# Unused matrix products in front of 31 of TensorE's waits, in a long one-core network kernel

## The chip, the cores and the metric

The kernel runs on one core of one Trainium2 chip, in one launch. The metric is the device time of that launch in microseconds (us), the median over its runs. TensorE (PE in the rows) does the matrix products, VectorE (DVE), ScalarE (ACT) and GpSimd (POOL) the rest; each works through its own instructions in order and waits on semaphores for the others.

## The reference

One batch of 512 positions with 1024 features goes through five layers. All arithmetic is fp32.

```python
# the first block (DEPTH = 1)
h = _rms(x, norm1_w[l]) * (1 + sc1) + sh1
x = x + g1 * _hybrid_mixer(h, ...)        # state-space scan + dilated attention + pooling
h = _rms(x, norm2_w[l]) * (1 + sc2) + sh2
x = x + g2 * (jnp.square(jax.nn.relu(h @ w_ff1[l])) @ w_ff2[l])
# the second block: four layers on 512 latent and 256 context positions
#   l = 0, 3: window attention;  l = 1: attention with low-rank q and kv;  l = 2: decayed attention
#   y_l, y_c = mixer(rmsnorm(h_l) ..., rmsnorm(h_c) ...);  each then normed, gated and added to x
def rmsnorm(x, g):
    xf = x.astype(jnp.float32)
    y = xf * lax.rsqrt(jnp.mean(xf * xf, axis=-1, keepdims=True) + EPS)
    return (y * g.astype(jnp.float32)).astype(x.dtype)
```

## The kernel before, in words

Most of the work is in `dense`: a weight matrix comes in 156 slots of 128x2048, each is split into a high part (ScalarE, line 409) and a low part (GpSimd, line 401), and each product of the reference becomes three products in TensorE's fp32r form (lines 414, 415 and 416: high by high, low by high, high by low). A tile of the output accumulates over 8 chunks of 128 features in one of the 8 PSUM banks and is taken out by ScalarE or VectorE. With `lead=2` the first two tiles of a call are built together, chunk by chunk, so that TensorE can begin when the first chunk of its input (`a_hi`, `a_lo`) has been written.

Between these calls stand stages in which TensorE has little to do:

- `pre_norm` squares each chunk of x on ScalarE (line 880), sums over the features with a product by a matrix of ones (line 896), takes the root on ScalarE (`root_rows`, lines 843 and 846, each with a load of a table), and scales and splits on VectorE and ScalarE (lines 919, 932, 905). In the second block it comes at the start of every layer, for the 512 latent columns and then the 256 context columns. `rms_scale` (lines 823 and 832) is its plain form, used twice in `ssd_out`.
- `layer_out` ends a layer: a dense product, a sum of squares (line 2239), and x plus the gated, normed y on VectorE (lines 2256 and 2264), chunk by chunk, with `pre_norm` of the next layer behind it.
- `ssd_branch` has four short stages with a barrier after each (`end_stage`: every engine drains, counts up a semaphore and waits for the others): transposes of dt (line 1046), transposes of the inputs (line 1069), the states (line 1126), and the heads (lines 1218, 1232, 1235).
- `dilated_attention` norms the heads (line 1350, ones by squares), and `group_attention` (line 1398: scores), `pair_attention` (lines 1671: scores, 1681: transposes, 1692: values), the attention of layer 1 (lines 1513 to 1536) and `decayed_attention` (lines 2936 to 2954) do the attentions.

The order on every engine is written out by hand. Products on plain fp32 operands are two instructions each in the trace (a count of x16 in a row is 8 products); those of lines 414 to 416 are one each.

## Time and profile before

| | |
|---|---|
| median of 3 runs | 3102.14 us (3098.28 to 3105.61) |
| the profiled execution's own time | 3101.86 us |
| its span, first to last instruction | 3100.1 us |
| TensorE busy | 2813.1 us (91%) |
| VectorE, ScalarE, GpSimd busy | 54%, 39%, 24% |
| mean granted TensorE clock | 0.958 of full speed |

The clock that the chip grants TensorE has two levels in the records, 1.00 (2.4 GHz) and 0.50 (1.2 GHz). A busy time of TensorE holds the work done at either. An idle time is written behind a row in brackets, with what ended it.

### The profile page before, as it was taken

The numbers are of one execution on the slowest core, as the hardware profiler recorded it, in microseconds if no ns is written. First come the engines' busy times: TensorE is split into PE (matmuls) and PEld (weight loads), VectorE is DVE, ScalarE is ACT, GpSimd is POOL, SyncE is SP. The second block draws the span as 40 slices with busy tenths as digits, with TensorE's granted clock in tenths as the row PEclk, the third lists the DMA queues.
The fourth block names the chain that finished last, engine by engine and source line by source line (L and its number), as shares of the span: only waits on it lengthen the run. The fifth ranks groups of instructions, "written<-read, shape, count | busy, mean of one in ns | idle before, by whom it ended". The sixth has DMA issues, their size and how long they took to land.

```text
span 3100.1 us, 39554 instructions
## 1 busy us (share of the span) xinstructions
PE 2813.1 (91%) x16088; PEld 2295.3 (74%) x16088; DVE 1674.2 (54%) x3104; ACT 1217.1 (39%) x2104; POOL 743.5 (24%) x160
## 2 busy tenths in 40 slices
PE   3978989989899999999989989999899999889896
PEld 1855877768687787769867768777689998768685
DVE  5877295162822999970088441354490248450583
ACT  3335224553223122242268354543443336352482
POOL 1411433403343344423200112100122210113101
PEclk7989999999899999999999999999999999989998
DMA  6412463302323554521100211101121331122101
GB/s 239 183 41 102 186 235 109 109 1 82 109 95 126 186 190 178 202 109 69 56 14 2 82 68 69 41 1 43 64 84 69 137 136 42 68 82 82 41 2 68
DMA packets 49620, 294.79 MB, mean 95 GB/s; under 512 B 4448, under 2 KB 5792, under 8 KB 19616
## 3 DMA queue, kind: packets, MB, share of 16 engines
q1 hardware_dynamic: 22464, 163.59, 14.6%
q10 hardware_dynamic: 26976, 128.68, 10.9%
q8 instruction: 128, 2.10, 0.3%
q14 instruction: 52, 0.43, 0.0%
HBM read 271.25 MB, written 21.00 MB: 94 GB/s over the span
## 4 chain that ended last, share of the span: by engine, by line
PE 63%; DVE 18%; ACT 4%; issue 3%; DMA 0%; ACTq 0%; DVEq 0%
PE psum L414 16%; PE psum L415 15%; PE psum L416 15%; DVE ada_temp L748 5%; PE psum L1671 2%; PE psum L896 2%; PE psum L2954 2%; PE psum L1513 2%; PE psum L1536 2%; PE psum L1692 1%; DVE pair_row L1721 1%; PE psum L1681 1%; PE psum L1517 1%; PE psum L1525 1%; DVE pair_prob L1730 1%
## 5 line engine op out<-in xcount | busy, mean ns | idle before, releaser
L401 POOL TENSOR_TENSOR w_lo<-raw,w_hi 128x2048 fp32r<-128x2048 f32 x156 | 743.3, 4765 | 2314.3 <-ACT w_hi L409 2314.3
L414 PE MATMUL psum<-a_hi,w_hi 128*128 128x512 f32 (+3 forms) x1880 | 708.1, 377 | 78.4 <-DVE a_lo L905 54.2
L415 PE MATMUL psum<-a_lo,w_hi 128*128 128x512 f32 (+3 forms) x1880 | 698.8, 372 | 0.0
L416 PE MATMUL psum<-a_hi,w_lo 128*128 128x512 f32 (+3 forms) x1880 | 698.1, 371 | 0.0
L414 PEld LDWEIGHTS psum<-a_hi,w_hi 128*128 128x128 f32 (+1 forms) x1880 | 356.7, 190 | 156.1 <-issue 56.8
L748 DVE SCALAR_TENSOR_TENSOR ada_temp<-ada_ring,ada_rows 128x1024 f32<-128x1024 f32 x240 | 426.7, 1834 | 78.8 <-ACT ada_rows L708 46.3
L415 PEld LDWEIGHTS psum<-a_lo,w_hi 128*128 128x128 f32 (+1 forms) x1880 | 357.2, 190 | 63.3 <-issue 4.2
L416 PEld LDWEIGHTS psum<-a_hi,w_lo 128*128 128x128 f32 (+1 forms) x1880 | 356.6, 190 | 63.3 <-issue 2.2
L409 ACT ACTIVATE w_hi<-raw 128x2048 fp32r<-128x2048 f32 x156 | 298.1, 1912 | 250.5 <-DMA raw<-stream 105.6
L414 PE MATMUL psum<-w_hi,a_hi 128*128 128x256 f32 x800 | 229.6, 287 | 0.5 <-ACT c_gate_rows L2830 0.5
L416 PE MATMUL psum<-w_hi,a_lo 128*128 128x256 f32 x800 | 226.3, 283 | 0.0
L415 PE MATMUL psum<-w_lo,a_hi 128*128 128x256 f32 x800 | 226.3, 283 | 0.0
L414 PEld LDWEIGHTS psum<-w_hi,a_hi 128*128 128x128 f32 x800 | 153.4, 192 | 2.4 <-issue 1.4
L415 PEld LDWEIGHTS psum<-w_lo,a_hi 128*128 128x128 f32 x800 | 153.5, 192 | 1.5 <-issue 1.4
L416 PEld LDWEIGHTS psum<-w_hi,a_lo 128*128 128x128 f32 x800 | 153.5, 192 | 0.0
L2226 DVE TENSOR_TENSOR square<-y 128x512 f32<-128x512 f32 (+1 forms) x56 | 44.8, 800 | 179.6 <-ACT y L2232 179.6
L1721 DVE CUSTOM_DVE_ANT_0 pair_row<-psum,pair_mask,neg_sinks 128x512 f32<-128x512 f32 (+2 forms) x160 | 116.6, 747 | 38.3 <-PE psum L1671 25.3
L1749 ACT ACTIVATE pair_prob<-pair_row,pair_stat 128x513 f32<-128x513 f32 (+2 forms) x160 | 114.8, 719 | 42.3 <-DVE pair_stat L1721 21.9
L896 PE MATMUL psum<-squares,const 128*128 128x512 f32 (+1 forms) x160 | 79.7, 658 | 39.6 <-ACT squares L880 39.3
L1671 PE MATMUL psum<-gk,gq 64*128 64x128 f32 (+1 forms) x960 | 98.7, 340 | 18.2 <-DVE pair_stat L1721 14.5
L414 PE MATMUL psum<-hid_hi,w_hi 128*128 128x512 f32 x256 | 102.5, 400 | 8.3 <-DVE hid_lo L598 8.3
L2232 ACT ACTIVATE y<-psum 128x512 f32<-128x512 f32 (+1 forms) x56 | 28.3, 506 | 202.8 <-PE psum L416 202.5
(386 smaller groups left out, 4647.1 us busy)
## 6 DMA issues: line engine op xcount, KB each, us to landing
raw<-stream SPq DMA_DIRECT2D x156, 1024.0 KB, 4.8
ada_ring<-ada ACTq DMA_DIRECT2D x72, 1024.0 KB, 5.7
xres<-x_in ACTq DMA_DIRECT2D x4, 3072.0 KB, 10.2
x_in<-xres ACTq DMA_DIRECT2D x3, 3072.0 KB, 11.5
gates<-gate_part ACTq DMA_DIRECT2D x8, 768.0 KB, 3.8
c_rows_m<-rows_m ACTq DMA_DIRECT2D x2, 1536.0 KB, 7.8
c_og<-gates ACTq DMA_DIRECT2D x4, 768.0 KB, 6.2
c_z<-gates ACTq DMA_DIRECT2D x4, 768.0 KB, 6.2
```

Source lines behind the costliest of these rows:

```text
L401: pool.tensor_tensor(k.w_lo[:, r], k.raw[:, r], k.w_hi[:, r].bitcast(F32), ALU.subtract) \
L409: act.activation(k.w_hi[:, r], k.raw[:, r], ACT.Copy).then_inc(k.hi_ready, 1)
L414: pe.matmul(out, lhs[0], rhs[0], start=start, stop=False)
L415: pe.matmul(out, lhs[0], rhs[1], start=False, stop=False)
L416: return pe.matmul(out, lhs[1], rhs[0], start=False, stop=stop)
L748: dve.scalar_tensor_tensor(self.temp[:, self.products % 2], self.ring[:, place, c], 1.0, self.rows[:, w], ALU.mult, ALU.mult, accum_out=se ...
L896: pe.matmul(k.psum[:, banks[n], 0:t1 - t0], k.cst("ones"), squares[:, i % 2, 0:t1 - t0], start=c == 0, stop=c == KC - 1).then_inc(summed.s ...
L1513: pe.matmul(score(u)[:, col:col + cols], q, keys, start=True, stop=False)
L1536: last = pe.matmul(value_bank(u), units[u]["pv"][j], prob_t[:, u % n_t, j * P:(j + 1) * P], start=j == 0, stop=j == n_blocks - 1)
L1671: last = pe.matmul(score(u)[:, col:col + cols], q, keys, start=True, stop=True)
L1721: dve.tensor_tensor_reduce(row[:, u % 4, 1:1 + w], score(u), mask[:, un["mask"]:un["mask"] + w], 1.0, un["sink"], ALU.add, ALU.min, stat[: ...
L1749: act.activation(prob[:, u % 4, 0:1 + width(u)], row[:, u % 4, 0:1 + width(u)], ACT.Exp, bias=stat[:, 0, u % 4:u % 4 + 1], scale=-1.0, acc ...
```

## The change

A new function `keep_busy` issues n products of the matrix of ones (128x128) by the first 256 columns of the constants, plain fp32, into a bank that is free; nothing reads them. It is called at 31 places of the built program, 199 products in all, 2 to 20 at a place, always in front of a wait of TensorE. Where the bank may still be in use, a wait for it is put ahead. No other engine's instructions change, and no real product is moved against another.

```diff
+    def keep_busy(self, pe, bank, n):
+        for _ in range(n):
+            pe.matmul(bank[:, 0:256], self.cst("ones"), self.const[:, 0:256], start=True, stop=True)
...
 # dense: new arguments fill=0, fill_end=0
                 if together:
                     pe.wait_ge(free.sem, free.at(together - ring))
+                    k.keep_busy(pe, bank(0), fill)
...
                     pe.wait_ge(free.sem, free.at(t + 1 - ring))
+                    if t == 0:
+                        k.keep_busy(pe, bank(t), fill)
...
+    if fill_end:
+        @block.tensor
+        def _(pe):
+            pe.wait_ge(free.sem, free.at(1 - n_banks))
+            k.keep_busy(pe, bank(total), fill_end)
...
 # rms_scale
+        k.keep_busy(pe, k.psum[:, banks[0], :], 5)
         for c in range(n_chunks):
             pe.wait_ge(sq.sem, sq.at(c + 1))
...
 # pre_norm: fill=(0, 0); (6, 6) in layers 1 to 3, (0, 6) in layer 0
         for i, (c, n, t0, t1) in enumerate(work):
+            if c == 0 and fill[n]:
+                pe.wait_ge(k.tile_free.sem, k.tile_free.at(0))
+                k.keep_busy(pe, k.psum[:, next(b for b in (2, 3, 4) if b not in banks), :], fill[n])
             pe.wait_ge(sq.sem, sq.at(i + 1))
...
 # ssd_branch: 11 after the dense product "xbc" (ahead of its barrier), then
+                k.keep_busy(pe, k.psum[:, 7, :], 2)
             last = pe.transpose(k.psum[:, 2, 16 * c:16 * c + 16], dt_rows[:, c * P:(c + 1) * P],
                                 k.cst("ident")[0:16, 0:16])
         last.then_inc(turned.sem, 1)
+        k.keep_busy(pe, k.psum[:, 7, :], 8)
...
+        k.keep_busy(pe, k.psum[:, 7, :], 5)
         for c in range(3):
             pe.wait_ge(ready.sem, ready.at(c + 1))
...
+        k.keep_busy(pe, k.psum[:, 5, :], 7)
         rows(0)
         rows(1)
...
 # the attention of layer 1, at its end
+        pe.wait_ge(masked.sem, masked.at(2 * n))
+        k.keep_busy(pe, k.psum[:, 0, :], 11)
...
 # pair_attention (layers 0 and 3)
             if p + 1 < n:
                 scores(p + 1)
+            if p < 2:
+                k.keep_busy(pe, k.psum[:, 7, :], 5)
             if p >= 3:
                 values(p - 3)
+        pe.wait_ge(masked.sem, masked.at(2 * n))
+        k.keep_busy(pe, k.psum[:, 0, :], 4)
...
 # dilated_attention, around the last head norms
+        k.keep_busy(pe, k.psum[:, 0, :], 6)
         for t in range(side.STEPS):
             side.on_tensor(pe, t)
+        k.keep_busy(pe, k.psum[:, 0, :], 11)
...
 # calls of dense: ff1_0 fill=10, ff2_0 fill=4, and fill=5 for A0q, Bin, Cqk and A3q
 # decayed_attention
+                if (h, c) == (H - 1, 0):
+                    k.keep_busy(pe, front(q), 20)
                 pe.wait_ge(normed.sem, normed.at(6 * h + 6))
...
+        pe.wait_ge(taken.sem, taken.at(N))
+        k.keep_busy(pe, acc(0, 0), 4)
```

On TensorE, from the end of layer 1 into layer 2, the program before reads (`total` is the sum of squares of y, `squares` that of x, `a` the input of the next dense product):

```order
L2239 MATMUL psum<-total_17733,const_52 128x256
L890 UNCONDITIONAL_BRANCH
L896 MATMUL psum<-squares_18354,const_52 128x512 x8
L896 MATMUL psum<-squares_18354,const_52 128x256 x8
L446 UNCONDITIONAL_BRANCH
L414 MATMUL psum<-a_hi_9963,w_hi_51 128x512
```

The same place on TensorE after the change (a line number is 6 to 32 higher, and line 352 is the new product):

```order
L2271 MATMUL psum<-total_17868,const_52 128x256
L906 UNCONDITIONAL_BRANCH
L352 MATMUL psum<-const_52 128x256 x6
L915 MATMUL psum<-squares_18489,const_52 128x512 x8
L352 MATMUL psum<-const_52 128x256 x6
L915 MATMUL psum<-squares_18489,const_52 128x256 x8
L453 UNCONDITIONAL_BRANCH
L352 MATMUL psum<-const_52 128x256 x5
L420 MATMUL psum<-a_hi_10040,w_hi_51 128x512
```

Three groups of new products have come in, one ahead of each of the three waits; the second stands ahead of the first of the eight narrow products, and the order of the others is as it was.

On TensorE in `ssd_branch`, after the change, the two stages of the states (`xd`) and the heads (`tri_a`) begin so:

```order
L1091 MATMUL psum<-const_52,xbc_605 128x128 x40
L365 UNCONDITIONAL_BRANCH
L1143 UNCONDITIONAL_BRANCH
L352 MATMUL psum<-const_52 128x256 x5
L1149 MATMUL psum<-xd_1663,b_tok_607 128x512 x6
L1155 MATMUL psum<-xbc_605 128x128 x8
L365 UNCONDITIONAL_BRANCH
L1234 UNCONDITIONAL_BRANCH
L352 MATMUL psum<-const_52 128x256 x7
L1241 MATMUL psum<-tri_a_1720,const_52 128x512 x3
```

Line 365 is the barrier, so here the new products stand behind a barrier, where before the first product of each stage stood.

## Rows read from the trace of the kernel before

**Rows 1.** The page: TensorE's busy time, and the chain that ended last.

```profile
PE 2813.1 (91%) x16088; PEld 2295.3 (74%) x16088; DVE 1674.2 (54%) x3104; ACT 1217.1 (39%) x2104; POOL 743.5 (24%) x160
PE 63%; DVE 18%; ACT 4%; issue 3%; DMA 0%; ACTq 0%; DVEq 0%
```

**Rows 2.** Windows (length, busy by engine, clock, DMA): 3 of 26 slow stretches, and their sum.

```profile
2224.94:2231.77 6.83, 5.81 (x7) 2.42 (x8) 6.83 (x13) 2.78 (x6) 0.00 (x0) 0.50 0.00 0
2242.01:2245.42 3.41, 3.41 (x9) 2.10 (x8) 0.00 (x0) 1.82 (x5) 0.00 (x0) 0.50 0.02 8
2259.07:2262.49 3.42, 3.42 (x11) 2.62 (x10) 3.42 (x10) 2.04 (x5) 0.00 (x0) 0.50 0.00 0
...
sum 167.30, PE 123.07 PEld 77.70 DVE 102.22 ACT 71.22 POOL 7.20; mean PE 4.73 PEld 2.99 DVE 3.93 ACT 2.74 POOL 0.28
```

**Rows 3.** Timeline of TensorE: products at 1.00, at 0.50, and 257 columns wide.

```profile
2254.10 0.39 PE L414 MATMUL psum<-a_hi,w_hi 128*128 128x512 f32 x1
2254.33 0.39 PE L415 MATMUL psum<-a_lo,w_hi 128*128 128x512 f32 x1
...
2260.10 0.63 PE L415 MATMUL psum<-a_lo,w_hi 128*128 128x512 f32 x1
2260.53 0.63 PE L416 MATMUL psum<-a_hi,w_lo 128*128 128x512 f32 x1
...
2644.68 7.97 PE L2954 MATMUL psum<-cv,c_decay 128*128 128x257 f32 x36
```

**Rows 4.** Timeline of TensorE from layer 1 into layer 2.

```profile
2225.96 10.80 PE L896 MATMUL psum<-squares,const 128*128 128x512 f32 x18 [3.62 <-ACT squares L880]
2240.38 5.46 PE L896 MATMUL psum<-squares,const 128*128 128x256 f32 x14 [3.62 <-ACT squares L880]
2246.51 0.47 PE L414 MATMUL psum<-a_hi,w_hi 128*128 128x512 f32 x1 [0.68 <-DVE a_lo L905]
...
2257.89 0.50 PE L414 MATMUL psum<-a_hi,w_hi 128*128 128x512 f32 x1 [2.94 <-DVE a_lo L905]
```

**Rows 5.** Timeline of VectorE and ScalarE there: last full-width x, last full-width square.

```profile
2231.65 0.69 DVE L2264 TENSOR_TENSOR x_in<-x_in,y 128x512 f32<-128x512 f32 x1
...
2234.52 0.63 ACT L880 ACTIVATE squares<-x_in 128x512 f32<-128x512 f32 x1 [0.42 <-PE psum L896]
```

**Rows 6.** Sum row of the 11 slow stretches at the layers' starts.

```profile
sum 54.64, PE 46.08 PEld 26.66 DVE 40.71 ACT 29.99 POOL 0.00; mean PE 4.19 PEld 2.42 DVE 3.70 ACT 2.73 POOL 0.00
```

**Rows 7.** Sum row of 6 slow stretches under dense products behind a wait.

```profile
sum 40.97, PE 27.11 PEld 20.69 DVE 22.00 ACT 12.03 POOL 4.56; mean PE 4.52 PEld 3.45 DVE 3.67 ACT 2.01 POOL 0.76
```

**Rows 8.** Sum row of the 7 slow stretches in the first block's short stages.

```profile
sum 51.21, PE 36.21 PEld 19.51 DVE 27.74 ACT 21.17 POOL 2.64; mean PE 5.17 PEld 2.79 DVE 3.96 ACT 3.02 POOL 0.38
```

**Rows 9.** Timeline of the first block: stages behind a barrier, on three engines.

```profile
211.17 1.42 DVE L1157 TENSOR_TENSOR cb<-psum,const 128x512 f32<-128x512 f32 x2 [0.53 <-DVEq L366]
...
213.36 2.71 PE L1218 MATMUL psum<-tri_a,const 128*128 128x512 f32 x4 [3.81 <-DVE tri_a L1164]
...
267.30 1.15 ACT L823 ACTIVATE squares<-z 128x512 f32<-128x512 f32 x2 [4.88 <-DVEq L366]
267.98 5.40 PE L832 MATMUL psum<-squares,const 128*128 128x512 f32 x8 [2.43 <-ACT squares L823]
...
277.00 6.54 PE L832 MATMUL psum<-squares,const 128*128 128x512 f32 x8 [3.62 <-ACT squares L823]
```

**Rows 10.** Transposes of the first block, and one stretch within them.

```profile
190.51 6.62 PE L1069 MATMUL psum<-const,xbc 128*128 128x128 f32 x40 [1.43 <-ACTq L371]
...
190.60:194.00 3.40, 3.40 (x17) 3.40 (x18) 1.92 (x4) 0.00 (x0) 0.00 (x0) 0.50 0.00 0
194.01:197.40 3.39, 3.12 (x25) 2.48 (x23) 3.39 (x7) 0.00 (x0) 0.00 (x0) 1.00 0.00 0
```

**Rows 11.** Timeline of TensorE at the start of the attention of layer 0.

```profile
1572.02 2.50 PE L1671 MATMUL psum<-gk,gq 64*128 64x128 f32 x16 [1.86 <-DVE pair_stat L1721]
1574.45 1.97 PE L1681 MATMUL psum<-const,pair_prob 128*128 128x128 f32 x8
```

More of the change, by code:

```diff
@@ L419, in dense @@
 def dense(k, block, sections, tiles, act_tile=None, dve_tile=None, act_last=None, turn_slots=None, ada=None,
-          barrier=True, n_banks=BANKS, side=None, lead=1):
+          barrier=True, n_banks=BANKS, side=None, lead=1, fill=0, fill_end=0):
     first = SECTIONS[sections[0]][0]
@@ L849, in pre_norm @@
 def pre_norm(k, block, x, a, parts, coef, shift, temp, part_ready=None, then=None,
-             at_end=None, before_chunk=None, after_root=None):
+             at_end=None, before_chunk=None, after_root=None, fill=(0, 0)):
     squares = k.at("squares", temp, [P, 2, S])
@@ L994, in ssd_branch @@
           dve_tile=conv_tile,
-          act_last=lambda act, i, t: act.activation(xbc[:, t, :], conv[:, t % 2], ACT.Silu))
+          act_last=lambda act, i, t: act.activation(xbc[:, t, :], conv[:, t % 2], ACT.Silu), fill_end=11)
     dt = k.at("dt", small, [P, 9, 64])
@@ L1045, in _ @@
         for c in range(4):
+            if c == 0:
+                k.keep_busy(pe, k.psum[:, 7, :], 2)
             last = pe.transpose(k.psum[:, 2, 16 * c:16 * c + 16], dt_rows[:, c * P:(c + 1) * P],
@@ L2087, in square @@
             return split(k, dve, hid[0][:, t, :], hid[1][:, t, :], ps)
-        dense(k, block, [f"ff1_{b}"], feature_major(a, KC, full), lead=2 if b == 0 else 1,
+        dense(k, block, [f"ff1_{b}"], feature_major(a, KC, full), lead=2 if b == 0 else 1, fill=10 if b == 0 else 0,
               act_tile=lambda act, i, t, ps: act.activation(r[:, t % 4, :], ps, ACT.Relu), dve_tile=square,
@@ L2096, in add_ff @@
                                             ALU.add)
-        dense(k, block, [f"ff2_{b}"], feature_major(hid, KC, full), dve_tile=add_ff, ada=ada.of(4), barrier=False)
+        dense(k, block, [f"ff2_{b}"], feature_major(hid, KC, full), dve_tile=add_ff, ada=ada.of(4), barrier=False, fill=0 if b else 4)
     modulation_end(k, block)
@@ L2145, in token_major, with layer_norm_in @@
     return tiles
-def layer_norm_in(k, block, l, a, x_at, temp, part_ready=None):
+def layer_norm_in(k, block, l, a, x_at, temp, part_ready=None, fill=(6, 6)):
     x = k.at("x_in", x_at, [P, KC, T2])
@@ L2163, in layer_norm_in @@
     pre_norm(k, block, x[:], a, [LAT, CTX], lambda n, c: k.coef2[:, l, c, n:n + 1],
-             lambda n, c: k.mod2[:, l, c, n:n + 1], temp, part_ready, save, saved)
+             lambda n, c: k.mod2[:, l, c, n:n + 1], temp, part_ready, save, saved, fill=fill)
     stored.stage_over(16)
@@ L2304, in gqa_layer @@
         k.context_in(block)
-        layer_norm_in(k, block, l, a, R0 + 32768, R0 + 90112, x_ready)
+        layer_norm_in(k, block, l, a, R0 + 32768, R0 + 90112, x_ready, fill=(0, 6))
     parts = [LAT, CTX] if both else [LAT]
@@ L2326, in gqa_layer @@
     dense(k, block, [f"A{l}q"], feature_major(a, KC, parts), turn_slots=2, act_tile=into(q, ACT.Copy, parts, -A_SCALE),
-          barrier=False, lead=2)
+          barrier=False, lead=2, fill=5)
     if not both:
@@ L2500, in into @@
         return put
-    dense(k, block, ["Bin"], feature_major(a, KC, both), act_tile=into(raw, ACT.Copy), barrier=False, lead=2)
+    dense(k, block, ["Bin"], feature_major(a, KC, both), act_tile=into(raw, ACT.Copy), barrier=False, lead=2, fill=5)
     steps = LatentSteps(k, raw, low, R0 + 36864)
@@ L2811, in place @@
         return 2 * (c % 4) + c // 4
-    dense(k, block, ["Cqk"], feature_major(a, KC, both), barrier=False, lead=2,
+    dense(k, block, ["Cqk"], feature_major(a, KC, both), barrier=False, lead=2, fill=5,
           act_tile=lambda act, i, t, ps: act.activation(pad[:, t % 8, 2:2 + span(t)[0]], ps[:, 0:span(t)[0]],
```

## Prediction

> **What bounds the kernel now.** I read the page first. TensorE is busy for 2813.1 us, and the chain that ended last runs through it for 63% of the span, through VectorE for 18% and ScalarE for 4% [rows 1]. So time taken off TensorE is as a rule time taken off the whole, but not everywhere.
>
> Then I asked at which clock TensorE did its work, and cut the span into windows at each step of the granted clock. Near the places of the change lie 26 stretches in which it was 0.50; together they last 167.30 us, and TensorE was busy for 123.07 us of that [rows 2]. What such a stretch costs is in the timeline of TensorE. At 1.00 one fp32r product 512 columns wide starts 0.23 us after the one before (2254.10 to 2254.33), at 0.50 it is 0.43 us (2260.10 to 2260.53) [rows 3]. Of work that is limited by TensorE, (0.43 - 0.23)/0.43 = 0.47 would be saved. The ceiling of this change is therefore 0.47 x 123.07 = 58 us, 1.9% of the time.
>
> Last I read what TensorE did before each fall. From layer 1 into layer 2 it idled for 3.62 us, and the clock was 0.50 from 2224.94; it idled for 3.62 us again, and it was 0.50 from 2242.01; it idled for 2.94 us, and it was 0.50 from 2259.07 [rows 2, 4]. The clock came back only in the midst of the dense work behind. The same three gaps stand at the start of layers 1 and 3. So the falls follow the idle time, and new products in it have something to prevent.
>
> **What a new product costs.** It is 128x256 in plain fp32, so two instructions. The nearest row is one of plain fp32 with 257 columns: 36 instructions in 7.97 us at 1.00, so 0.22 us each [rows 3], and 0.43 to 0.44 us for a product. All 199 are 86 us at 1.00 and, at half the clock, 172 us. They are free as long as they end before the awaited event, since no other engine waits for them, and nothing but TensorE's own queue stands behind them.
>
> **The layers' starts (layer 2 worked out).** First gap: six products, 2.6 us, in 3.62 us of idle time. They fit, and about 1 us of idle time is left. The eight squares behind it: VectorE has the last full-width x at 2231.65 + 0.69 = 2232.34, while ScalarE only ends the last square at 2234.52 + 0.63 = 2235.15, since it waits for TensorE [rows 5]. A square takes 0.63; at 1.00 it would be done at about 2233.0. Saved: 2.1 us. Second gap: six more, 2.6 of 3.62 us. The narrow products behind it, 14 instructions, take 5.46 us mostly at 0.50 [rows 4]. At 1.00 one costs 0.43 with a square of about 0.4 in turns with it on two buffers, some 0.55 to 0.6 us a product, 4 us in all. Saved: 1.5 us. Third: five products, 2.2 us, stand in front of a dense product that waited only 0.68 us [rows 4], so it begins some 1.0 to 1.5 us later than it could. But eleven microseconds on TensorE waits 2.94 us for a late `a_lo`, which comes from ScalarE and VectorE [rows 4]; the lateness is taken out of that wait, which shrinks to under 2 us. I expect that the fall at 2259.07 goes with it, and its 3.42 us of dense work [rows 2] gives 1.6 us. Layer 2 in all: 5.2 us for 5.81 + 3.41 + 3.42 = 12.64 us of slow busy time [rows 2], 0.41 for each. The eleven stretches of this kind, in four layers, hold 46.08 us [rows 6]: 18.9 us.
>
> **Dense products behind a wait.** Six stretches (ff1_0, ff2_0, the ends of the four attentions) hold 27.11 us [rows 7]; the new products stand in gaps that are longer than they are. At 0.47 this is 12.7 us. I take off 2.7 us: in ff2_0 the chunks of its input come from VectorE one by one, and the 12 transposes at the end of layer 2 sit between steps of the other engines. That leaves 10.0 us.
>
> **The first block's short stages.** Seven stretches hold 36.21 us [rows 8], at 0.47 17.0 us. But here the products can be late. Behind a barrier TensorE can't begin them during the gap before it. For the heads VectorE leaves the barrier at 211.17 and the first sum is released at 213.36 [rows 9]: 2.2 us for seven products, which take 3.0 us, so 0.8 us late. In front of the first `rms_scale` the square begins at 267.30, right behind the barrier, and the sum at 267.98 [rows 9]: 0.7 us for five products of 2.2 us, 1.4 us late (its 5.40 us for 8 instructions then become 8 x 0.43 = 3.5 us, the pitch of a 512-column plain fp32 instruction being twice the 0.22 us of 257 columns, so that a little is still won; the second group of sums, 6.54 us to 3.5 us, wins 3 us [rows 9]). With the same reckoning at the state stage (five, 0.7 us), the dt transposes (two, 0.9 us) and the head norms (six behind a barrier, 1.5 us) I take off 5.3 us, and 1.3 us more for steps where another engine is waited for. That leaves 10.4 us.
>
> At this place a rule of the skill speaks against part of it. The 40 transposes run from 190.51 to 197.13; the clock was 0.50 until 194.00 and 1.00 from 194.01, with nothing but transposes on TensorE in those 3.4 us [rows 10], so these transposes do raise the clock. The Trainium skill, "TensorE: Matmul & The Clock Gate", Part 4, says that transpose-mode products do not count as TensorE being busy for the clock. By the rule the clock would fall again under these transposes, and 1 to 2 us of the sum would go; by that rule, the trace disagrees, and I leave the sum as it is.
>
> **The start of pair attention (layers 0 and 3).** Here five products stand behind the second scores and five behind the third, and the two gaps ahead of them are not filled. In layer 0 the clock is already 0.50 when the first group starts, so it takes up to 4.3 us in a gap of 1.86 us; the second group stands in front of transposes that waited for nothing (1572.02 + 2.50 against 1574.45) [rows 11]. Up to 4 us late, against an earlier return of the clock. I take -0.5 us for each of the two layers, with bounds of -4 and +2.
>
> **The sum.** 18.9 + 10.0 + 10.4 - 1.0 = 38.3 us. It takes every fall as prevented. The clock does not step at the same places of the program in each execution, and some 1 us of idle time stays in most gaps, so I take off a tenth: 34 us. The profiled execution's own time is 3101.86 us, 0.3 us under the median: 3101.9 - 34 = 3068 us.
>
> **Rivals.**
>
> *Most falls go, but the path is elsewhere (3080 to 3095 us, 16%).* Squares, roots and table loads on ScalarE and x on VectorE set the pace between the gaps; if only half of the slow busy time is on the path, 0.5 x 34 = 17 us are left, 3085 us. For it: VectorE's 18% of the chain. Against it: at the layers' starts ScalarE's squares were ended by waits for TensorE (0.42 us ahead of the last one) [rows 5].
>
> *All falls go, and less is late than I reckon (under 3056 us, 14%).* 47 to 55 of the ceiling of 58 us. It needs the removal of falls that are not filled too, or the new wait times to be all hidden.
>
> *No change (3096 to 3108 us, 5%).* The rest of the gaps, 1 to 1.5 us each, plus the work at the edge, is still too little and the clock falls as before; the products end in time. Against it: the clock stayed up at gaps like the 0.68 us one, and through stretches with many short waits.
>
> *Slower (5%).* One mechanism: the new products run at 1.2 GHz and end late. Each then takes 0.86 us; over the 31 places their time less the gap that they stand in comes to about 65 us (for instance 6 x 0.86 - 3.62 = 1.5 us at each of the layers' starts, and 7 x 0.86 - 2.2 = 3.8 us at the heads [rows 4, 9]), and nothing is won: 3167 us. A place that goes this way loses about 2 us and its gain of 1.1 us; with a third of the products at 0.50 the change is worth nothing, and above that it costs. Against it: the products of ones by squares, the same operands in kind, stood alone on TensorE when the clock rose under them at 2231.77 [rows 2, 4], so such products keep it up. Most of the new ones begin right behind busy stretches, at 1.00.
>
> **How the numbers follow.** My forecast, 3056 to 3080 us, has 60%, its own value 3068 us. With the neighbours on either side as the rivals have them, 3052 to 3090 us leaves out the no-change and slower cases (10%) and the outer parts of the first two rivals (about 8%). A measurement of this kernel can tell about 0.2%, 6 us, from no change: faster 90%, same 5%, slower 5%.
>
> **What the profile of the changed kernel would show.** The mean granted clock up from 0.958 to about 0.98; rows of the new products with about 0.22 us for each instruction; the narrow products of the layers' starts in 4 us in place of 5.46 us; the wait for `a_lo` there under 2 us in place of 2.94 us; the sums of `rms_scale` in 3.5 us each, the first of them released by TensorE itself and not by ScalarE. The first two hold even if the gain fails; with them right and the time above 3085 us, the step "time off TensorE is time off the whole" is wrong. The prediction as a whole is wrong if stretches at 0.50 remain behind the filled gaps, or if the new products show a pitch of 0.43 us for each instruction.

## Result: 0.7% faster, three fifths of what was forecast

The changed kernel takes 3082.76 us (median of 4 runs, 3078.56 to 3083.55), the kernel before on the same chip 3103.88 us (4 runs, 3098.28 to 3107.87). The ratio is 0.9933, 95% interval 0.9922 to 0.9945: 20.8 us less (0.0067 x 3103.88, and 17 to 24 us by the interval), where 34 us were forecast. The time lies 2.8 us above my band of 3056 to 3080 us and inside the wider 3052 to 3090 us. The profiled execution took 3083.36 us, with a span of 3081.5 us and a mean granted clock of 0.976, up from 0.958.

The page of the changed kernel (busy time with instructions; the chain that ended last, by engine) answers to [rows 1]:

```profile
PE 2867.7 (93%) x16486; PEld 2352.0 (76%) x16486; DVE 1676.5 (54%) x3104; ACT 1217.4 (40%) x2104; POOL 745.1 (24%) x160
PE 61%; DVE 20%; ACT 3%; issue 3%; DMA 1%; DVEq 0%; ACTq 0%; PEldq 0%; PEld 0%
```

TensorE has 398 more instructions (199 products) and is busy for 54.6 us more, and yet the whole is shorter. The chain moved by two points from TensorE to VectorE: at some places TensorE is no longer what the others wait for.

The windows of the changed kernel at steps of the granted clock, those behind places of the change (length, busy time by engine, clock, DMA share, GB/s), answer to [rows 2]:

```profile
625.72:635.96 10.24, 8.35 (x18) 4.86 (x18) 4.80 (x23) 2.11 (x5) 0.00 (x0) 0.50 0.00 1
1554.14:1564.38 10.24, 8.57 (x38) 6.60 (x38) 5.65 (x19) 4.61 (x9) 0.00 (x0) 0.50 0.00 0
...
2212.91:2216.33 3.42, 3.42 (x10) 2.70 (x9) 3.42 (x7) 3.26 (x6) 0.00 (x0) 0.50 0.28 115
...
sum 44.39, PE 39.23 PEld 28.77 DVE 31.52 ACT 23.57 POOL 0.00; mean PE 4.90 PEld 3.60 DVE 3.94 ACT 2.95 POOL 0.00
```

Eight stretches at 0.50 are left there, with 39.23 us of busy time, of 26 with 123.07 us. A ninth (1042.14 to 1045.56, 3.42 us busy) is in `ff2_0`, where one of the 26 stood too; the others stand at places that the change does not touch. So some 80 us of slow busy time went. At 0.47 this would be 38 us; 20.8 us came out, 0.26 for each. The question is where the rest stayed.

TensorE from layer 1 into layer 2 in the changed kernel, the rows that answer to [rows 4] (L352 are the new products, L915 the squares' sums):

```profile
2211.73 0.70 PE L2271 MATMUL psum<-total,const 128*128 128x256 f32 x2 [1.96 <-DVEq L372]
2212.26 4.44 PE L352 MATMUL psum<-const 128*128 128x256 f32 x12
2216.54 7.72 PE L915 MATMUL psum<-squares,const 128*128 128x512 f32 x16
2224.10 2.75 PE L352 MATMUL psum<-const 128*128 128x256 f32 x12
...
2228.38 4.49 PE L915 MATMUL psum<-squares,const 128*128 128x256 f32 x14 [1.09 <-ACT squares L896]
2232.71 2.32 PE L352 MATMUL psum<-const 128*128 128x256 f32 x10
2234.68 0.58 PE L420 MATMUL psum<-a_hi,w_hi 128*128 128x512 f32 x1
...
2245.16 0.50 PE L420 MATMUL psum<-a_hi,w_hi 128*128 128x512 f32 x1 [1.93 <-DVE a_lo L924]
```

VectorE's last full-width x and ScalarE's last full-width square there, two timelines, answer to [rows 5]:

```profile
2221.73 0.69 DVE L2296 TENSOR_TENSOR x_in<-x_in,y 128x512 f32<-128x512 f32 x1
```

```profile
2222.46 0.63 ACT L896 ACTIVATE squares<-x_in 128x512 f32<-128x512 f32 x1 [0.35 <-DVE x_in L2296]
```

Count from the end of the last full-width x, 2222.42 (2232.34 before). ScalarE's last square ends 0.67 us behind it, 2.81 before. The narrow sums begin after 5.96 us (8.04 before) and end after 10.45 us (13.50 before); the dense product begins after 12.26 us (14.17 before), and the product behind the wait for `a_lo` after 22.74 us (25.55 before). So 2.1 us were won in front of the narrow sums and 1.0 us in them; 1.1 us of that was given back in front of the dense product, and at the next wait 2.8 us are left. The square is now awaited from VectorE and not from TensorE. Two more things show in the rows. The first six products ran almost wholly at half the clock, 4.44 us, since it had fallen (2212.91) behind a gap of 1.96 us ahead of them, which the change does not fill. And the last five ran without any idle time behind them: they were late.

### The profile page after: what moved, and what is told of

Same layout as the page of the kernel before. It is cut to its first block, busy times and chain, and to the rows that moved or that the text cites. A ratio compares the mean times of both kernels' runs of the same rounds, so it can differ in the third digit from the quotient of the medians.

```text
span 3081.5 us, 40346 instructions
## 1 busy us (share of the span) xinstructions
PE 2867.7 (93%) x16486; PEld 2352.0 (76%) x16486; DVE 1676.5 (54%) x3104; ACT 1217.4 (40%) x2104; POOL 745.1 (24%) x160
## 4 chain that ended last, share of the span: by engine, by line
PE 61%; DVE 20%; ACT 3%; issue 3%; DMA 1%; DVEq 0%; ACTq 0%; PEldq 0%; PEld 0%
PE psum L420 15%; PE psum L421 15%; PE psum L422 15%; DVE ada_temp L763 5%; PE psum L1697 2%; PE psum L2988 2%; PE psum L1537 2%; PE psum L1560 2%; PE psum L1718 1%; DVE pair_row L1751 1%; PE psum L1707 1%; DVE y L2288 1%; PE psum L1541 1%; DVE a_lo L924 1%; DVE x_in L2296 1%
## 5 line engine op out<-in xcount | busy, mean ns | idle before, releaser
L352 PE MATMUL psum<-const 128*128 128x256 f32 x398 | 99.9, 405 | 9.2 <-ACTq L377 5.8
## 6 DMA issues: line engine op xcount, KB each, us to landing
x_in<-xres ACTq DMA_DIRECT2D x3, 3072.0 KB, 10.2
```

The source lines that it names most:

```text
L352: pe.matmul(bank[:, 0:256], self.cst("ones"), self.const[:, 0:256], start=True, stop=True)
```

## Experiments

Each was timed in five rounds beside the kernel before. "Against the changed kernel" is the difference of the ratios times 3102 us; with intervals of about 0.0012 on either side it is known to about 5 us, so I give the difference of the profiled spans (3081.5 us) beside it. That is one execution on each side: the four spans of the changed kernel itself run from 3076.7 to 3081.7 us.

There is a finer reading. TensorE has the same 16088 real products in every kernel, so the start of one of them can be compared between two traces, just ahead of a place and just behind it. What the difference grows by is what the place is worth in these two executions, and "at the place" means this below. It shows two things that are in every difference of spans and have nothing to do with the edit. Ahead of the first new product, at 175 us, the traces are already up to 1.3 us apart. And a fall of the clock that one execution has and the other has not, at a place that is the same in both, moves all behind it by some 1.5 to 2 us.

Unless it is said otherwise, every kernel computes the whole reference.

**Is it the clock?** The same 199 products, 16 columns wide.

```
-            pe.matmul(bank[:, 0:256], self.cst("ones"), self.const[:, 0:256], start=True, stop=True)
+            pe.matmul(bank[:, 0:16], self.cst("ones"), self.const[:, 0:16], start=True, stop=True)
```

> All 199 new products stay in place, but each is 16 columns wide in place of 256. If the gain comes from the clock that the array's work keeps up, the clock falls as in the kernel before: mean granted clock 0.955 to 0.962, time 3097 to 3105 us. If any instruction on TensorE keeps the clock up (the loads of the ones matrix are all still there), clock 0.97 and above and 3075 to 3085 us.

Measured: 3106.5 us, ratio 1.001 (1.0001 to 1.0019), clock 0.956. Timeline of TensorE at the same place:

```profile
2224.80 1.41 PE L352 MATMUL psum<-const 128*128 128x16 f32 x12
2228.48 10.39 PE L915 MATMUL psum<-squares,const 128*128 128x512 f32 x16 [2.28 <-ACT squares L896]
```

As many instructions and weight loads as in the changed kernel, but 1.41 us of work in the gap and 2.28 us of idle time behind. The clock is as low as before, the wide sums take 10.39 us, and all of the gain is gone. So the gain comes through the clock, and instructions that take 1.41 us of such a gap don't bring it. Whether many more narrow ones, enough to fill the gap, would do it was not tried: the work of a product and the time that it takes are not told apart here.

**The start of pair attention: the products there taken out.**

```
-            if p < 2:
-                k.keep_busy(pe, k.psum[:, 7, :], 5)
```

> The change without its two groups of five at the start of pair attention in layers 0 and 3. In the changed kernel the other engines fell back there by 2.7 and 1.2 us against the kernel before. If the products there are only late (they ran at 0.50), this kernel is 2 to 4 us faster than the change, 3079 to 3081 us. If they pay by bringing the clock back earlier, it is 1 to 3 us slower, 3084 to 3086 us.

Measured: 3079.27 us, ratio 0.9928 (0.9915 to 0.994): 1.6 us faster than the changed kernel (span 3077.0, 4.5 us less; at the two places 2.5 and 1.4 us). They cost. The changed kernel's timeline of TensorE in layer 0 shows why, beside [rows 11]:

```profile
1554.22 2.09 PE L1697 MATMUL psum<-gk,gq 64*128 64x128 f32 x12 [1.78 <-DVEq L372]
1557.90 2.51 PE L1697 MATMUL psum<-gk,gq 64*128 64x128 f32 x16 [1.59 <-DVE pair_stat L1751]
1560.34 4.41 PE L352 MATMUL psum<-const 128*128 128x256 f32 x10
1564.67 1.37 PE L1697 MATMUL psum<-gk,gq 64*128 64x128 f32 x16
1565.97 2.43 PE L352 MATMUL psum<-const 128*128 128x256 f32 x10
```

The clock fell at 1554.14, behind the gap of 1.78 us. The five products begin after two unfilled gaps, take 4.41 us at 0.50 in a gap of 1.86 us, and make the third scores some 2.4 us late (see the next experiment); the next five stand in front of transposes that waited for nothing.

**The same place, filled from its first gap.**

```
             pe.matmul(k.psum[:, n % 2, :], k.cst("swap"), c, start=True, stop=True).then_inc(swapped.sem, 1)
+        k.keep_busy(pe, k.psum[:, 2, :], 3)
...
         scores(0)
+        k.keep_busy(pe, k.psum[:, 7, :], 3)
...
-            if p < 2:
-                k.keep_busy(pe, k.psum[:, 7, :], 5)
+            if p == 0:
+                k.keep_busy(pe, k.psum[:, 7, :], 3)
```

> The five products behind the second and the five behind the third scores of pair attention are gone. Instead three stand at the end of the rotation, ahead of its barrier (bank 2), three behind the first scores and three behind the second, so that the two gaps of about 1.9 us are filled from their start. Theory (the old ones came late and at 0.50 because the clock had already fallen in the gaps ahead of them): the stretch at 0.50 at 1554 us goes, and that at 2888 us too; the 10 us and 7.7 us of slow busy time there are worth up to 3 us more than leaving the old products out, so a ratio to before of 0.9915 to 0.992 (3076 to 3078 us), against 0.9928 without any. Rival (work there is set by VectorE's and ScalarE's steps, and products in short gaps are only late): no better than without any, 0.9925 to 0.9935.

Measured: 3072.74 us (4 runs), ratio 0.9908 (0.9895 to 0.9922), span 3070.8: 7.8 us faster than the changed kernel by the ratios, 10.7 by the spans, 5.6 and 4.0 us at the two places. Better than the theory's range, and the rival falls. Its timeline of TensorE, and one window:

```profile
1552.33 1.46 PE L352 MATMUL psum<-const 128*128 128x256 f32 x6
1554.27 1.26 PE L1697 MATMUL psum<-gk,gq 64*128 64x128 f32 x12 [0.48 <-DVEq L372]
1555.46 1.56 PE L352 MATMUL psum<-const 128*128 128x256 f32 x6
1557.62 1.37 PE L1697 MATMUL psum<-gk,gq 64*128 64x128 f32 x16 [0.59 <-DVE pair_stat L1752]
1558.92 1.56 PE L352 MATMUL psum<-const 128*128 128x256 f32 x6
1560.85 1.37 PE L1697 MATMUL psum<-gk,gq 64*128 64x128 f32 x16 [0.37 <-DVE pair_stat L1752]
```

```profile
1550.20:1562.00 11.80, 10.15 (x66) 6.75 (x66) 9.22 (x25) 4.62 (x9) 0.00 (x0) 1.00 0.00 0
```

Nine products in place of ten, every gap filled from its start, none late: the stretch runs at 1.00. From the first scores to the third it is 6.6 us (1554.27 to 1560.85), against 10.5 in the changed kernel (1554.22 to 1564.67) and 8.1 in the kernel without any products there (1553.41 to 1561.47).

**The layers' first gap left empty** (layers 1 to 3, 18 products less).

```
-def layer_norm_in(k, block, l, a, x_at, temp, part_ready=None, fill=(6, 6)):
+def layer_norm_in(k, block, l, a, x_at, temp, part_ready=None, fill=(0, 6)):
```

> The change without the six products ahead of the wide squares of layers 1 to 3, which in the changed kernel ran at 0.50 from the first to the last and ended about 0.6 us late. If what they bring is the clock being back for the squares behind them, leaving them out costs 1 to 2 us for each layer: 3086 to 3089 us. If lateness and gain cancel, 3081 to 3084 us.

Measured: 3087.68 us, ratio 0.9954 (0.9941 to 0.9966): 6.5 us slower than the changed kernel (span 3086.7, 5.2 us more; at the three places 5.2 us together). The wide sums take 9.47 us in its timeline, against 7.72. Even at half the clock these products pay.

**The same gap bridged**: three products more ahead of the closing barrier, so that the six behind run at 1.00.

```
-          dve_tile=add_square, side=early)
+          dve_tile=add_square, side=early, fill_end=3 if following is not None else 0)
```

> The change with three more products at the end of each layer's last dense product (layers 0 to 2), ahead of its barrier, in an idle time of 1.97 us that the change leaves open and after which the clock fell in all three layers. If that gap makes the six products behind it run at 0.50, they now run at 1.00 (0.22 us for each instruction), the squares behind them start 0.6 us earlier: 1 to 4 us faster than the change, 3079 to 3082 us. If the fall has another cause, or the barrier gets late, 3083 to 3086 us and still 0.43 us for each instruction.

Measured: 3082.07 us, ratio 0.9935 (0.9923 to 0.9948), span 3082.0: nothing gained. Its timeline of TensorE, and of ScalarE:

```profile
2210.37 1.46 PE L352 MATMUL psum<-const 128*128 128x256 f32 x6
...
2212.71 2.75 PE L352 MATMUL psum<-const 128*128 128x256 f32 x12
2216.40 8.31 PE L915 MATMUL psum<-squares,const 128*128 128x512 f32 x16 [0.94 <-ACT squares L896]
```

```profile
2222.90 0.63 ACT L896 ACTIVATE squares<-x_in 128x512 f32<-128x512 f32 x1 [0.37 <-DVE x_in L2296]
```

The fall at 2212.91 is gone, the six take 2.75 us in place of 4.44, and 0.94 us of idle time returns. But the wide sums now take 8.31 us in place of 7.72: their last squares wait for VectorE's x, at the same place behind it as in the changed kernel. VectorE sets the end here, so a faster TensorE brings nothing more.

**The second gap left empty** (ahead of the last parts' squares, all four layers).

```
-def layer_norm_in(k, block, l, a, x_at, temp, part_ready=None, fill=(6, 6)):
+def layer_norm_in(k, block, l, a, x_at, temp, part_ready=None, fill=(6, 0)):
```

> Without the six products in the second gap (ahead of the last parts' squares) of each of the four layers' starts; the first six and the dense product's five stay. My prediction took 1.5 us a layer for this gap, 6 us in all: ratio to before 0.9952. Theory now (the narrow products at 1.00 end 1.0 us earlier, but VectorE and ScalarE with h and a_hi follow and the dense product starts by its own five late): half of it or less, 0 to 4 us slower than the changed kernel, 0.9933 to 0.9946. Rival (the clock would fall in this gap and stay at 0.50 into the dense product, as before the change): 6 us or more, 0.9952 or above.

Measured: 3087.59 us, ratio 0.9947 (0.9935 to 0.996): 4.3 us slower than the changed kernel (span 3087.4, 5.9 us more; at the four places 3.9 us together, the rest of the span's difference is falls elsewhere). This lies between theory and rival, and does not decide between them. In its timeline the narrow sums take 6.07 us against 4.49:

```profile
2231.22 6.07 PE L915 MATMUL psum<-squares,const 128*128 128x256 f32 x14 [3.67 <-ACT squares L896]
```

**Nothing in front of the first dense product.**

```
-          barrier=False, lead=2, fill=5)
+          barrier=False, lead=2, fill=0)
```

> Without the five products in front of the first dense product of each of the four layers. Theory (they make that product 1.1 us late and do not keep the clock up: it still fell behind the wait for a_lo in layers 1 and 3): as fast as the changed kernel or up to 3 us faster, ratio to before 0.9923 to 0.9935, with the wait for a_lo back at 2.9 us and the clock falling behind it in all four layers. Rival (as I predicted, the lateness is taken out of the wait for a_lo and the fall goes, 1.6 us in a layer): 4 to 6 us slower than the changed kernel, 0.9946 to 0.9953.

Measured: 3082.45 us, ratio 0.9939 (0.9925 to 0.9952): 1.9 us slower than the changed kernel by the ratios, 2.7 us shorter by the spans, so no difference that these runs can tell. Product by product there is none: ahead of the start and behind the wait for `a_lo` the two traces are apart by the same amount within 0.1 us, in each of the four layers. The 2.7 us come from the clock at 1554 and 1977 us, where both kernels are the same: the changed kernel's execution has a longer stretch at 0.50 at the first and the only one at the second, 1.6 us each. From that go 0.5 us that arose before 175 us. Timeline of TensorE in layer 2:

```profile
2225.67 4.49 PE L915 MATMUL psum<-squares,const 128*128 128x256 f32 x14 [1.09 <-ACT squares L896]
2231.08 0.47 PE L420 MATMUL psum<-a_hi,w_hi 128*128 128x512 f32 x1 [0.92 <-DVE a_lo L924]
...
2242.45 0.50 PE L420 MATMUL psum<-a_hi,w_hi 128*128 128x512 f32 x1 [2.93 <-DVE a_lo L924]
...
2243.25 0.40 PE L420 MATMUL psum<-a_hi,w_hi 128*128 128x512 f32 x1
2243.49 0.39 PE L421 MATMUL psum<-a_lo,w_hi 128*128 128x512 f32 x1
```

From the start of the narrow sums the dense product begins after 5.41 us, against 6.30 in the changed kernel; the product behind the wait for `a_lo` after 16.78 us in both (2242.45 - 2225.67, 2245.16 - 2228.38). The 0.9 us of lateness is indeed taken out of that wait, as I predicted, and nothing else comes of it: behind the wait the clock falls in layers 1 and 3 with the five products and without, and in layers 0 and 2 in neither (the pitch behind it is 0.24 us).

**The dense products behind a wait** (ff1_0, ff2_0, the ends of the attentions; 57 products less).

```
-        dense(k, block, [f"ff1_{b}"], feature_major(a, KC, full), lead=2 if b == 0 else 1, fill=10 if b == 0 else 0,
+        dense(k, block, [f"ff1_{b}"], feature_major(a, KC, full), lead=2 if b == 0 else 1,
...
-        pe.wait_ge(masked.sem, masked.at(2 * n))
-        k.keep_busy(pe, k.psum[:, 0, :], 11)
...
-                if (h, c) == (H - 1, 0):
-                    k.keep_busy(pe, front(q), 20)
```

> Without the 57 products in front of dense products behind a wait: ff1_0 (10), ff2_0 (4), the ends of the two pair attentions (4 each), of layer 1's attention (11), and layer 2's output (20 and 4). My prediction took 10.0 us for them: ratio to before 0.9965. Theory (these are in time and TensorE is what the rest waits for; by the shift of the other engines between the two traces they brought 1.9, 1.2, 1.6, 1.5 and 3.1 us, 9.3 in all): 8 to 10 us slower than the changed kernel, 0.9959 to 0.9965. Rival (the shifts were the noise of one execution, and the clock soon comes back anyway): 3 to 5 us, 0.9943 to 0.9949.

Measured: 3093.65 us (9 runs), ratio 0.9977 (0.9967 to 0.9986): 13.6 us slower than the changed kernel (span 3092.2, 10.7 us more). The first group in this kernel and in the changed one:

```profile
982.89 0.76 PE L420 MATMUL psum<-a_hi,w_hi 128*128 128x512 f32 x1 [5.73 <-DVE a_lo L924]
983.45 0.63 PE L421 MATMUL psum<-a_lo,w_hi 128*128 128x512 f32 x1
983.88 0.63 PE L422 MATMUL psum<-a_hi,w_lo 128*128 128x512 f32 x1
```

```profile
976.11 4.48 PE L352 MATMUL psum<-const 128*128 128x256 f32 x20
981.91 0.50 PE L420 MATMUL psum<-a_hi,w_hi 128*128 128x512 f32 x1 [1.32 <-DVE a_lo L924]
982.24 0.39 PE L421 MATMUL psum<-a_lo,w_hi 128*128 128x512 f32 x1
982.47 0.40 PE L422 MATMUL psum<-a_hi,w_lo 128*128 128x512 f32 x1
```

Ten products end 1.32 us before `a_lo` comes, and the dense product goes on at a pitch of 0.23 us in place of 0.43. At this place TensorE is the bound behind the wait, and the whole 0.47 comes out: 2.6 us for the 5.6 us that TensorE is busy there at 0.50. (A new fall in the changed kernel, 1008.01, takes 0.9 us of it back.) At the ends of layers 1, 2 and 3 it is 2.5, 3.3 and 2.9 us. The four products of `ff2_0` bring nothing: they run from 1031.31 to 1033.20, where TensorE had no idle time, and the wait for `hid_lo` comes behind the third chunk. Nor do those at the end of layer 0. All in all 9.4 us at the places.

**The first block's short stages** (49 products less: dt, states, heads, the sums of `rms_scale`, head norms).

```
-        k.keep_busy(pe, k.psum[:, 5, :], 7)
...
-        k.keep_busy(pe, k.psum[:, banks[0], :], 5)
```

> Without the 49 products of the first block's short stages (dt, states, heads, both sums of rms_scale, head norms); the 11 ahead of group attention stay. My prediction took 10.4 us for them: ratio to before 0.9967. Theory now (5.6 us of lateness against what the clock gives back, by the shift of the other engines up to 613 us): 2 to 4.5 us slower than the changed kernel, 0.994 to 0.9948. Rival (they are worth nothing): 0.9933.

Measured: 3084.46 us, ratio 0.9934 (0.9922 to 0.9947): 0.3 us slower than the changed kernel (span 3084.8, 3.3 us more; at the places 4.0 us together). The ratio is the rival's and the traces are the theory's; with 5 us of uncertainty the ratio can't decide, and the 10.4 us are outside of both. Its sums in `rms_scale`, and those of the changed kernel:

```profile
265.70 5.40 PE L847 MATMUL psum<-squares,const 128*128 128x512 f32 x8 [2.43 <-ACT squares L838]
274.71 6.70 PE L847 MATMUL psum<-squares,const 128*128 128x512 f32 x8 [3.62 <-ACT squares L838]
```

```profile
266.41 3.73 PE L848 MATMUL psum<-squares,const 128*128 128x512 f32 x8
...
273.85 3.83 PE L848 MATMUL psum<-squares,const 128*128 128x512 f32 x8 [1.56 <-ACT squares L838]
```

At the first sums the changed kernel begins 0.7 us later here and ends 1.0 us earlier (270.14 against 271.10); at the second ones it ends 3.7 us earlier (277.68 against 281.41). TensorE ends its last product of the heads at 262.33 in the changed kernel and at 263.27 in this one, so the 33 products in front of that (dt, states, heads) brought 0.9 us of it (1.1 with the 0.2 us that the traces are apart at 175 us), and the pair of `rms_scale` stages 2.8.

The 10.4 us of the prediction held more than these 49 products. The last of its seven stretches, 9.87 us of busy time out of 36.21, is group attention, and the 11 products ahead of that stay in this kernel. What they bring shows in the changed kernel:

```profile
624.87 0.94 PE L1422 MATMUL psum<-qkv 128*128 128x128 f32 x6 [1.90 <-DVEq L372]
```

They end 1.9 us before the barrier does, and the clock falls behind that (625.72, the first of the windows above). Of the 4.6 us that 0.47 x 9.87 put into the sum nothing came; from 600 to 645 us the changed kernel even falls back 0.4 us against the kernel before.

**Fewer behind the barriers, some ahead of them.**

```
+        k.keep_busy(pe, k.psum[:, 7, :], 3)
...
-        k.keep_busy(pe, k.psum[:, 7, :], 5)
+        k.keep_busy(pe, k.psum[:, 7, :], 2)
...
-        k.keep_busy(pe, k.psum[:, 5, :], 7)
+        k.keep_busy(pe, k.psum[:, 5, :], 5)
...
+        k.keep_busy(pe, k.psum[:, 5, :], 3)
...
-                  banks=((k.bank_at + g) % BANKS,))
+                  banks=((k.bank_at + g) % BANKS,), fill=5 if g else 1)
...
+              n_banks=6, side=side, fill_at={"end": 5} if j == 3 else None)
...
-        k.keep_busy(pe, k.psum[:, 0, :], 6)
+        k.keep_busy(pe, k.psum[:, 0, :], 2)
```

> Behind four barriers of the first block there are fewer of the new products (states 5 to 2, heads 7 to 5, first sum of rms_scale 5 to 1, head norms 6 to 2), and some ahead of the barriers (3, 3 and 5, in time that TensorE waits for the others). Theory (in the changed kernel these products end 1.1, 1.0, 1.7 and 1.8 us after what the real work needs is there, so 5.6 us are lost): 3 to 5 us faster than the changed kernel, ratio to before 0.9917 to 0.9925. Rival (the lateness lies in the slack of VectorE's and ScalarE's own chains, or the clock falls again with fewer products behind): within 1.5 us of the changed kernel, 0.993 to 0.9938.

Measured: 3077.97 us, ratio 0.9923 (0.9911 to 0.9936), span 3075.4: 3.1 us faster than the changed kernel by the ratios, 6.1 by the spans. (Of the products ahead, three stand before the states' barrier, three before that of `rms_scale`, five before the head norms.) Timeline of TensorE at `rms_scale`:

```profile
262.99 0.70 PE L352 MATMUL psum<-const 128*128 128x256 f32 x2 [0.35 <-DVEq L372]
263.59 3.83 PE L857 MATMUL psum<-squares,const 128*128 128x512 f32 x8
```

The idle time at the barrier is 0.35 us in place of 1.82, and the sum follows 0.6 us behind the barrier, not 2.3. Here the lateness was real, and 1.5 us are won and kept. At the states and heads it is the rival that holds. TensorE's sums of the heads come 1.7 us earlier, but then the clock falls (214.6), as it did not in the changed kernel. The heads' first products in this kernel, and in the changed one:

```profile
214.62 0.62 PE L1269 MATMUL psum<-ea,h_prev 128*64 128x128 f32 x2
```

```profile
217.43 0.38 PE L1259 MATMUL psum<-ea,h_prev 128*64 128x128 f32 x2
```

By 225 us nothing of the 1.7 us is left. (In the last kernel below, with the same products here, this fall does not come and 0.8 us stay.) And 2.2 us more are won in group attention, at 3.4 us of 0.50 in place of 10.2 behind the same wait of 1.9 us, with the same 11 products. So the time came out in the theory's range, and of the 5.6 us of lateness 1.5 to 2 are shown.

**More gaps.**

```
-        k.keep_busy(pe, k.psum[:, 0, :], 11)
+        k.keep_busy(pe, k.psum[:, 0, :], 15)
...
-    dense(k, block, ["mix"], mix_tiles, dve_tile=scaled, barrier=False)
+    dense(k, block, ["mix"], mix_tiles, dve_tile=scaled, barrier=False, fill_at={(1, 6): 8})
...
+          out_parts, {(j, 2): (k.tile_free.sem, k.free_of[j]) for j in range(KC)}, fill=17)
...
+            if self.fill:
+                pe.wait_ge(self.logs.sem, self.logs.at(0))
+                k.keep_busy(pe, k.psum[:, 7, :], self.fill)
```

> Four gaps more are filled: the products ahead of group attention are 15 in place of 11 (the gap of 1.9 us behind them), 14 in the 7.4 us gap at 494 us, 8 in the 4.3 us gap at 818 us, 17 in the 9.0 us gap at 826 us. The stretches at 0.50 behind these gaps hold 22.4 us of busy time. Theory (time off TensorE is time off the whole there too): 0.47 of it, 10 us faster than the changed kernel, ratio 0.990. Rival (behind a gap that long TensorE isn't what the others wait for: the group attention and the pooling branch go by VectorE): 2 to 5 us, 0.9917 to 0.9927.

Measured: 3084.55 us, ratio 0.9944 (0.9931 to 0.9956), span 3083.0: slower than the changed kernel by 3.4 us (1.5 by the spans), so neither theory's number. The edit was wrong, not only its size. Timeline of TensorE:

```profile
817.88 6.23 PE L352 MATMUL psum<-const 128*128 128x256 f32 x16 [4.33 <-DVE m_lo L622]
823.76 0.58 PE L420 MATMUL psum<-m_hi,w_hi 128*128 128x512 f32 x1
...
844.69 7.50 PE L352 MATMUL psum<-const 128*128 128x256 f32 x34
851.84 0.59 PE L420 MATMUL psum<-x_hi,w_hi 128*128 128x512 f32 x1
```

I had put the eight behind a wait for a free bank that ends when the gap of 4.33 us ends, and the seventeen in front of the third tile of a stage whose first one holds the gap. Both groups ran behind their gaps and were late in full, 5.9 and 7.2 us. The next wait of TensorE swallowed the first lateness whole; the second came out as 7.6 us. So this run says nothing of these two gaps. The other two places were right (2.3 us at 494 us; 3.6 us at group attention, where a gap of 0.36 us is left and the clock stays at 1.00), and went into the next kernel.

**Together**: three products in each of the three first gaps of pair attention, the barriers' version above, 15 ahead of group attention, 14 in the 7.4 us gap of the head norms at 494 us.

> Together: three products each in the three gaps at the start of pair attention from their beginning, none behind (9 us faster than the changed kernel when alone); fewer behind four barriers of the first block and some ahead (3 us alone); 15 in place of 11 ahead of group attention and 14 in the gap at 494 us (4.5 us up to 633 us alone, by the trace). If the gains are at places of their own they add: 15 to 17 us under the changed kernel, ratio to before 0.988 to 0.9885, 3066 us. Rival (a gain in front of the first block is taken back at the modulation rows, whose transfers set the pace there): only the part behind counts, 0.9905 to 0.991.

Measured: 3063.22 us (4 runs, 3061.79 to 3064.79), ratio 0.9869 (0.9854 to 0.9885), span 3060.0, clock 0.980. The gains add, against the rival: 19.9 us below the changed kernel, a little more than the 15 to 17 us expected. It is 41 us faster than the kernel before (0.0131 x 3104.92), twice what the change brought.

## Why the prediction held in its sign and was too high in its size

Each term against what its products are worth (the kernel without them, by ratio, by span and at the places). The 18.9 us of the layers' starts are split by the values worked out for layer 2:

| term | forecast, us | by ratio | by span | at the places |
|---|---|---|---|---|
| first gaps, layers 1 to 3 (3 x 2.1) | 6.3 | 6.5 | 5.2 | 5.2 |
| second gaps, 4 layers (4 x 1.5) | 6.0 | 4.3 | 5.9 | 3.9 |
| the fall behind the wait for `a_lo` (4 x 1.6) | 6.4 | 1.9 | -2.7 | 0.0 |
| dense products behind a wait | 10.0 | 13.6 | 10.7 | 9.4 |
| the first block's short stages (the forecast with the 11 ahead of group attention, the measures without) | 10.4 | 0.3 | 3.3 | 4.0 |
| the start of pair attention | -1.0 | -1.6 | -4.5 | -3.9 |
| sum | 38.1 | 25.0 | 17.9 | 18.6 |

The changed kernel stands in every row, so an error of its own ratio or span counts six times in a sum; that the measured 20.8 us lies between the first two proves little. The last column is the least disturbed. Beside it, the changed kernel's span is 18.6 us shorter than that of the kernel before, of which 1.3 us arose before the first new product.

- *The mechanism* was right: narrow products with the same count of instructions won nothing. The clock (0.976 against "about 0.98") and the price of a product at 1.00 (0.22 to 0.23 us for each instruction) came as said. But by the prediction's own sign it is wrong as a whole: stretches at 0.50 do remain behind filled gaps, eight or nine of 26, and new products ran at half the clock (4.41 us for the ten instructions at 1560.34, 4.44 for the twelve at 2212.26).
- *The layers' first gap* was right, 2.1 us by the squares' ends, 1.7 to 2.2 by the run without it. It was right although I had missed the gap of 1.97 us ahead of it: the clock falls there, and the six products are spent at half of it. That costs nothing only because VectorE's x sets the end, as the bridged version shows. The other half of my sum, the narrow products "in 4 us", took 4.49 us, so 1.0 us was won there and not 1.5.
- *"I expect that the fall at 2259.07 goes with it"* failed. The wait did shrink, from 2.94 to 1.93 us, under the 2 us that I had said. In layers 0 and 2 there was no fall behind it; in layers 1 and 3 there still was. And without the five products the same wait was 2.93 us in layer 2 with no fall either. They bring nothing, where 6.4 us were in the sum: one of the two large misses.
- *The dense products behind a wait* were right, 9.4 to 13.6 us for 10.0. The 2.7 us that I took off are about what `ff2_0` would have given (0.47 x 5.19 = 2.4 us), and it gave nothing.
- *The first block's short stages* are the other term that failed, 10.4 us in the sum and 0.3 to 4.0 on the chip. What was wrong is the 17.0 us at 0.47. Of these, 4.6 stood for group attention, where the fall was not prevented. The 33 products of dt, states and heads brought 0.9 to 1.1 us, and only the two sums of `rms_scale` came near to what I had reckoned there, 2.8 us for 1.9 - 1.4 + 3. The lateness, 5.3 us taken off, is shown for `rms_scale` (1.5 us got back, for 1.4); the rest of what the version with products ahead of the barriers won does not lie at those barriers. Which engine bounds each of the small stages was not tried one by one; the chain's shift to VectorE, 18% to 20%, is argument and not proof.
- *Pair attention* I had priced at -0.5 us a layer with bounds of -4 and +2, and the products there cost 1.6 to 4.5 us for both layers, 3.9 at the places. The sign and mechanism of the "up to 4 us late" were right; I had chosen the value too near to zero. I had written that "the two gaps ahead of them are not filled", and did not see what it meant: with those filled, the same place is worth 6.2 us (0.9908 against 0.9928 without any).
- The *tenth* taken off for falls that remain was too little: new falls came at unfilled places (1977.39, behind a wait of 2.06 us in layer 1), and 39.23 us of slow busy time stayed behind filled ones. Of the latter, 8.35 us are group attention's.
- Of the rivals, "most falls go, but the path is elsewhere" (3080 to 3095 us) holds the measured 3082.76 us. It is right for the first block and the wait for `a_lo`, and wrong as a rule: in the dense parts time off TensorE was time off the whole.

## What to carry to other kernels

In this kernel filling TensorE's waits paid where three things held: what stands behind the wait is bound by TensorE; the first of a row of gaps is filled, since gaps of 1.78 and 1.96 us left open made the products in the next one slow, and at pair attention late; and the products stand where the idle time begins (ahead of a barrier, not behind it), last until shortly before the awaited event, and end before it. Group attention is the plain case of the last: the 11 products of the changed kernel left 1.9 us and won nothing, 15 left 0.36 us and won 3.6. Price such a change place by place, by the engine that the work behind the gap waits for at full clock, and not by a share of all slow time. And read where in its queue a filler lands: one that runs behind its gap wins nothing, and costs its length unless a later wait swallows it (7.6 us for seventeen, nothing for eight).

## What the hardware did that I had not expected

- Twelve instructions of 16 columns took 1.41 us with their weight loads, and the clock was no higher for them (0.956 over the span, against 0.958). Loads that take so little of a gap of 3.6 us don't keep it up; loads that fill it were not tried.
- Gaps of 1.8 to 2.0 us were enough for a fall at several places (2212.91 behind 1.96 us, 1554.14 behind 1.78 us), while behind a wait of 1.93 us at 2245.16, and of 2.93 us at 2242.45 in the kernel without the five, it stayed at 1.00. I could not tell the two kinds apart from the length of the gap.
- A fall can come or go with no change at its place. In layer 1's attention the changed kernel had one at 1977.39, behind a wait of 2.06 us; with only the starts of pair attention repaired, the same wait of 2.06 us stood there and the clock was 1.00 from 1965 to 1980. Such a fall is worth 1.6 us of the whole, as much as several of the effects that were looked for.
